# Eight squares added on VectorE ahead of one sum on TensorE, and the convolution's mean one step later, in a two-kind transformer stack

## The reference

```
def rms_norm_2(x, g, eps=1e-6):
    y = x * lax.rsqrt(jnp.mean(x * x, axis=-1, keepdims=True) + eps)
    return y * g

for i in range(2):
    h = x + 0.5 * swiglu(rms_norm_2(x, norm_ffn1[i]), w_ffn1_in[i], w_ffn1_out[i])
    u = rms_norm_2(h, norm_mix[i])
    q, k, v, c, g = jnp.split(u @ w_in[i], splits, axis=-1)
    ...
    y_attn = window_attention(q, k, v, sink[i], rel_bias) @ w_attn_out[i]
    c = c_val * jax.nn.sigmoid(c_gate)
    c = depthwise_conv(c, conv_w[i], conv_b[i])
    c = jax.nn.silu(layer_norm_2(c, conv_ln_g[i], conv_ln_b[i]))
    y_conv = c @ w_conv_out[i]
    h = h + (g_attn * y_attn + g_conv * y_conv) @ w_o[i]
    h = h + 0.5 * swiglu(rms_norm_2(h, norm_ffn2[i]), w_ffn2_in[i], w_ffn2_out[i])
    x = h + (p[i] @ w_pe_proj[i]) * jax.nn.sigmoid(rms_norm_2(h, norm_pe[i]) @ w_pe_gate[i])
```

## Time and profile before

| what | value |
|---|---|
| median of 3 runs | 2180.13 us (2177.9 to 2181.48) |
| the profiled execution's own time | 2180.48 us |
| its span, first to last instruction | 2178.4 us |
| mean granted TensorE clock | 0.999 |
| PE busy | 2154.0 us, 99% |
| DVE busy | 1677.4 us, 77% |
| ACT busy | 1264.3 us, 58% |
| HBM read | 409.42 MB, 189 GB/s over the span |

### The profile page before, as it was taken

The page is one execution under the profiler, slowest core; times in us unless marked ns, Lnnn a source line. Parts: engine busy times, 40 slices in busy tenths (PEclk is TensorE's granted clock), DMA queues, the critical chain, the costliest instruction groups (busy, mean ns, idle before and its releaser), DMA issues.

```text
span 2178.4 us, 38806 instructions
## 1 busy us (share of the span) xinstructions
PE 2154.0 (99%) x16092; PEld 1968.2 (90%) x16092; DVE 1677.4 (77%) x2609; ACT 1264.3 (58%) x2098; POOL 13.1 (1%) x20
## 2 busy tenths in 40 slices
PE   7999999999999999999999999999999999999999
PEld 6898999998998998998888999988898889998888
DVE  7877589887876678876787677888678766978875
ACT  4744656554755556555555557566565545676554
POOL 0000000000000000000000000000000000000000
PEclk9999999999999999999999999999999999999999
DMA  9544566777644467655555533555555554355554
GB/s 371 182 157 167 169 241 233 251 246 267 232 146 156 151 226 225 212 175 185 184 189 188 184 121 115 202 193 189 188 176 192 189 188 136 117 165 204 192 189 131
DMA packets 116225, 415.10 MB, mean 191 GB/s; under 512 B 13089, under 2 KB 16289, under 8 KB 115538
## 3 DMA queue, kind: packets, MB, share of 16 engines
q1 hardware_dynamic: 116050, 412.63, 56.4%
HBM read 409.42 MB, written 3.16 MB: 189 GB/s over the span
## 4 chain that ended last, share of the span: by engine, by line
PE 94%; DVE 2%; ACT 2%; DMA 2%; issue 0%; SPq 0%; ACTq 0%
PE bank L198 93%; DMA raw<-W 1%; ACT arena L250 1%; PE bank L202 1%; DVE arena L205 1%; DVE lo L205 1%; DMA xT<-x 0%; ACT hi L250 0%; DVE ada L222 0%; ACT L242 0%; DVE arena L213 0%; ACT L250 0%; DVE h L205 0%; SPq L195 0%; DVE ysl L205 0%
## 5 line engine op out<-in xcount | busy, mean ns | idle before, releaser
L198 PE MATMUL bank<-h,hi 128*128 128x256 f32 (+1 forms) x5344 | 1224.3, 314 | 0.0
L250 ACT ACTIVATE hi<-raw 128x1024 fp32r<-128x1024 f32 x656 | 689.1, 1056 | 572.6 <-PE bank L198 512.0
L198 PE MATMUL bank<-h,lo 128*128 128x256 f32 x3440 | 986.6, 287 | 2.9 <-DVE h L205 2.8
L198 PEld LDWEIGHTS bank<-h,hi 128*128 128x128 f32 x5344 | 881.3, 191 | 67.2 <-issue 2.6
L205 DVE TENSOR_TENSOR lo<-raw,hi 128x1024 fp32r<-128x1024 f32 x656 | 793.4, 1221 | 93.0 <-ACT hi L250 92.1
L198 PEld LDWEIGHTS bank<-h,lo 128*128 128x128 f32 x3440 | 655.3, 191 | 14.7 <-issue 7.1
L198 PE MATMUL bank<-act,hi 128*128 128x512 f32 x1056 | 370.0, 393 | 0.0
L198 PE MATMUL bank<-act,lo 128*128 128x256 f32 x1056 | 294.7, 279 | 0.0
L198 PEld LDWEIGHTS bank<-act,hi 128*128 128x128 f32 x1056 | 197.9, 187 | 47.2
L198 PE MATMUL bank<-arena 64*64 64x64 f32 (+7 forms) x2674 | 197.4, 271 | 3.0 <-ACT arena L250 2.7
L198 PEld LDWEIGHTS bank<-act,lo 128*128 128x128 f32 x1056 | 197.9, 187 | 0.0
(11 more groups left out here) (150 smaller groups left out, 1913.8 us busy)
## 6 DMA issues: line engine op xcount, KB each, us to landing
raw<-W SPq DMA_DIRECT2D x664, 512.0 KB, 3.4
ada<-WA SPq DMA_DIRECT2D x80, 512.0 KB, 3.6
arena<-WA SPq DMA_DIRECT2D x16, 512.0 KB, 14.6
p_projected<-arena SPq DMA_DIRECT2D x2, 1024.0 KB, 7.9
arena<-scr SPq DMA_DIRECT2D x16, 128.0 KB, 4.8
arena<-p_projected SPq DMA_DIRECT2D x2, 1024.0 KB, 4.9
xT<-x SPq DMA_DIRECT2D x2, 512.0 KB, 5.8
arena<-lora SPq DMA_DIRECT2D x2, 512.0 KB, 10.9
```

Of the source, the lines that this page charges most:

```text
L198: return self.done(lambda e: e.matmul(out, l, r, start=start, stop=stop, skip_group_check=True))
L250: return self.done(lambda e: e.activation(out, in_, f, scale=scale, **kw))
```

## The change

For the eight norms of the second kind DVE adds all eight squares: `summed(norm)` is 7 for them and stays 5 for the others. After the lower half of tile 7 DVE adds square 6 and then square 7 (for the first `f1`, also those of the final norm). On PE, `squares` then has a single matmul for such a norm, and a single one for the final norm. Only the last matmul of a sum now signals. In the convolution's chain, "mean" and all that follows it come one tick later.

```diff
+def summed(norm):
+    return 7 if norm and norm[0] in ("f1", "mx", "f2", "pl") else SUMMED
...
-    return s + ["next", ("mean",), "next", ("square",), "next", ("var",), "next", ("norm",), ("silu",), "next", ("split",)]
+    return s + ["next", "next", ("mean",), "next", ("square",), "next", ("var",), "next", ("norm",), ("silu",), "next", ("split",)]
...
-            def squares(norm, parts, final=False):
+            def squares(norm, final=False):
+                parts = ["sum"] + list(range(summed(norm) + 1, KD))
                 for m in parts:
-                    if m in (0, "sum"):
+                    if m == "sum":
                         take(STAT, ("stat", norm))
...
-                    pe.mm(statb[:, 0:256], C("ones"), src, m in (0, "sum"), m == 7).then_inc(pe_main, ("stat", norm, m))
+                    i = pe.mm(statb[:, 0:256], C("ones"), src, m == "sum", m == parts[-1])
+                i.then_inc(pe_main, ("stat", norm))
                 if final:
-                    for m in parts:
-                        if m == "sum":
-                            take(ONE, "stat2")
-                            pe.wait_ge(v_main, "fsq sum")
-                        else:
-                            pe.wait_ge(a_main, ("fsq", m))
-                        src = t256(ht, 0 if m == "sum" else m)
-                        pe.mm(adab[:, 256:512], C("ones"), src, m == "sum", m == 7).then_inc(pe_main, ("stat2", m))
+                    take(ONE, "stat2")
+                    pe.wait_ge(v_main, "fsq sum")
+                    pe.mm(adab[:, 256:512], C("ones"), t256(ht, 0), True, True).then_inc(pe_main, "stat2")
...
-                if norm and 2 <= m <= SUMMED + 1:
+                if norm and 2 <= m <= summed(norm) + 1:
                     add_square(norm, m - 1)
+                if m == summed(norm) == KD - 1:
+                    add_square(norm, m)
...
-                    v_main, ("sq part", norm, m), *([("sq sum", norm)] if m == SUMMED else []))
+                    v_main, ("sq part", norm, m), *([("sq sum", norm)] if m == summed(norm) else []))
```

More of the change, by code:

```diff
@@ L1128, in tensor_program @@
                     pe.wait_ge(v_main, ("start sq", 256))
-                    pe.mm(statb[:, 0:256], C("ones"), t256(sqb, 0), True, True).then_inc(pe_main, ("stat", norm, 7))
+                    pe.mm(statb[:, 0:256], C("ones"), t256(sqb, 0), True, True).then_inc(pe_main, ("stat", norm))
                     start()
@@ L1135, in tensor_program @@
                     p_proj(l, [0])
-                    squares(("n1", l), ["sum", 6, 7])
+                    squares(("n1", l))
                     p_proj(l, [1, 2, 3])
@@ L1206, in tensor_program @@
                         flips(ONE, [0])
-                    squares(("n2", l), ["sum", 6, 7])
+                    squares(("n2", l))
                     if l == 0:
@@ L1230, in tensor_program @@
                     ffn_in(i, l, [0, 1], [(k, n) for k in range(KD) for n in range(4)])
-                    squares((f"f{i}", l), ["sum", 6, 7], (i, l) == (1, 0))
+                    squares((f"f{i}", l), (i, l) == (1, 0))
                 elif what == "f":
@@ L1245, in tensor_program @@
                     if m == 0:
-                        squares(("mx", l), ["sum", 6, 7])
+                        squares(("mx", l))
                 elif what == "rcol":
@@ L1289, in tensor_program @@
                     if m == 0:
-                        squares(("pl", l), ["sum", 6, 7])
+                        squares(("pl", l))
             assert f.n == NBLK * BT, f.n
@@ L1410, in add_square @@
                     v.tt(t256(ht, 0), t256(ht, 0), t256(ht, m), ADD).then_inc(
-                        v_main, ("fsq part", m), *(["fsq sum"] if m == SUMMED else []))
+                        v_main, ("fsq part", m), *(["fsq sum"] if m == summed(norm) else []))
             def updates(kind, l, p, nk):
@@ L1864, in vector_program @@
                             v.wait_ge(v_main)
-                            v.wait_ge(pe_main, ("stat2", 7))
+                            v.wait_ge(pe_main, "stat2")
                             v.tt(var_t, var_t, adab[:, 256:512], MUL).then_inc(v_main, "final var", frees="stat2")
@@ L2041, in factor @@
             def factor(norm):
-                a.wait_ge(pe_main, ("stat", norm, 7))
+                a.wait_ge(pe_main, ("stat", norm))
                 a.act(var_t, statb[:, 0:256], ACT.Ln, bias=C("eps6")).then_inc(a_main, ("ln", norm), frees=("stat", norm))
```

## The result

The changed kernel takes 2186.96 us (median of 7 runs, 2186.52 to 2189.03), the kernel before 2179.67 (7 runs): 1.0033 times as long, with a 95% interval from 1.0024 to 1.0042. It is 7.3 us slower, and outside the range given. The span of the profiled executions goes from 2178.4 to 2185.2 us.

What follows compares the result with a forecast made beforehand. PE, busy 99% of the span, was taken to bound the kernel. 7.8 us gained from sums, less 0.7 at `pl` and 7.3 at the tails, gave -0.2: forecast 2180.7 us, no change, range 2173.5 to 2185.

Steps and rivals of the forecast that it cites:

- 18 x 0.433 = 7.8 us off PE: At eight norms and the final norm, two float32 sums each leave PE, 0.433 us apiece, 7.8 us in all.
- work taken off PE counts in full: Premise for the whole kernel: with PE busy 99% of the span, any work removed from it shortens the time fully.
- The tail's 7.3 us: Convolution's tail one tick later: PE waits 4.8 us per layer in place of 1.15, 7.3 more for two layers.
- at the variance: First tail wait, inside attention's projection: PE waits 0.76 us for DVE's variance sums in place of 1.15.
- at the projection: Second tail wait, at the convolution's projection: late ACT table loads delay the first lower half, PE waits 2.9 us.
- at its second piece: Convolution's projection, after 6 matmuls: PE waits 0.9 us more for the second lower half.
- in the output product: DVE leaves the tail late and costs PE 0.2 us a layer at the output product's fifth lower half.
- DVE late at the output product: Slower rival: DVE carries the tail's lateness into the output product, 2.4 us a layer, 2185.5 us; chance 0.14.
- `pl`'s wait: At the `pl` norm the sum waits for DVE's two adds: 0.35 us in each of two layers, 0.7.
- One load for Ln and Exp: Rival in the convolution's tail: Ln's table load serves Exp too, 1.28 us shorter a layer, 2178.1 us; chance 0.07.
- no loads: Rival in the convolution's tail: Ln and Exp find their table, 2.56 us shorter a layer, 2175.5 us; chance 0.12.

Runs made afterwards that it cites:

- squares_only: The changed kernel with the convolution's mean put back to its earlier tick, so only the squares differ from the kernel before; 2178.6 us, ratio 0.9996.
- two_sums_only: Changed kernel, mean at its earlier tick, six squares added and two float32 sums at the three norms with slow FFN stretches; 2174.51 us, ratio 0.9976.
- mean_only: The kernel before with only the convolution's mean one tick later, squares and sums as before; 2189.61 us, ratio 1.0044.
- table_late: The changed kernel with ACT's table request moved from behind the square to ahead of Ln; 2179.75 us, ratio 1.0002 to the kernel before.
- more_sums: The changed kernel with dummy sums on PE, making two, three and four ahead of the three slow FFN stretches; 2184.63 us, ratio 1.0021.

## Why the prediction was wrong

- **"18 x 0.433 = 7.8 us off PE"** is the step that failed. The sums are off PE: the mixer's norm takes 0.25 from its first record to the next ordinary matmul (1231.94 to 1232.19) where it took 1.11 (1233.87 to 1234.98). But the step, and the premise "work taken off PE counts in full" ahead of it, took for granted that what PE does behind a sum takes as long as before. In three FFN stretches it doesn't: 3 x 2.1 = 6.3 us given back at places where no engine waits. squares_only (1.0 us gained of 7.1 forecast) and two_sums_only (5.0, with three sums left standing) show it from both sides. That the same matmuls have a second pace stood in the trace of before, where no wait and no count shows it: PE's first kind of block has it (rows in the last section).
- **The tail's 7.3 us** was right term by term where the clock stayed up, in layer 1. Lost time ahead of a matmul, beyond a step of 0.12: 0.73 at the variance (1353.07 - 1352.22; 0.76 forecast); in layer 1, 2.64 at the projection (1935.41 - 1932.65; 2.9), 0.77 at its second piece (1936.96 - 1936.07; 0.9) and 0.2 in the output product (0.2). With 0.2 for the slower first matmuls behind the waits that is 4.5, and 3.4 without the 1.15 of before, where 3.65 was forecast. Layer 0 lost 3.9. That the two come to 7.3 to the tenth is luck, for layer 0 has 0.5 of the clock in it; by medians the later mean costs 8.4 beside the squares (2186.96 - 2178.6) and 10.0 without them. The rival nearest in time, DVE late at the output product (2185.5), isn't what happened: PE lost 0.2 there, not 2.4.
- **The clock** was not in the forecast. In layer 0 it fell for 3.4 us, but in that time PE reached its second piece so late that the second wait was gone, so that it cost 3.9 - 3.4 = 0.5 there. In mean_only the fall came later, towards the end of the second wait, and a tail cost 4.5, 1.1 more than without a fall.
- **`pl`'s wait** was right: the last product's matmul starts at 1589.42, the sum at 1589.91, 0.37 beyond a step of 0.12, and 0.49 in layer 1 (2159.64 to 2160.25); 0.35 forecast. The other norms show no wait.
- **One load for Ln and Exp.** The Trainium skill (ScalarE: Activation LUTs, section "Table sets: the hidden batching unit") has one load serve Ln and then Exp. The trace differs where Ln brings its own load: Exp brings another (1356.45 and 1358.24). It agrees where the set with both was requested right ahead (table_late). So the rule's condition here is who asked for the set, and the rival "no loads" was one moved line away: the chance it got was for the change as written, where the loads came.

Together, by the starts: tails 3.9 + 3.4 = 7.3, pace 6.3, sums with the waits at `pl` -6.7 (read at each norm, some 0.87 less for every two sums), and the -0.2 from ahead of the second kind of block: the 6.8 of the spans. The forecast had 7.3 and -7.1 and no third term.

Open is what in PE makes the second pace. Shown is that one float32 sum ahead of an FFN stretch brought it in 15 of 17 and two or more never did at a stretch's start; that DVE's work, the clock and the sum's place by one matmul have no part in it; that a sum midway can end it or leave it; and that it also comes with no sum near. Whether it is the number of sums or the time for which they hold PE (0.43 us, or 0.87 and more) no run tells apart. What tells the two exceptions in table_late from the rest was not found; chance from one execution to the next isn't ruled out, for a product that is the same in all kernels here also came at either pace.

## What to carry to other kernels

Where PE is 99% busy, work taken off it counts only if the matmuls around it keep their pace: compare the distance of starts over a whole stretch in both traces, not only waits and counts. A step moved in ACT's order can put another function between a requested table and its use; move the request with it. And a wait of PE may cost more than itself: behind those of 2.5 us the clock fell in four tails of six.

## What the runs showed of the hardware that was not expected

- The same alternation of 128x256 and 128x512 float32r matmuls runs at one of two paces, 346.7 or 353.3 ns a tile, at a granted clock of 1.00 in both, and keeps one for 300 tiles. It isn't bound to this change, nor to float32 sums: in the first kind of block, where nothing was changed, the last 55 of the 64 tiles of layer 0's output product (`wout`) follow a wait for DVE and no sum. They ran at 353.3 to 353.4 in five of the twelve profiles, that of the kernel before among them, and at 346.7 in the others. PE's timeline before:

```profile
318.01 0.38 PE L198 MATMUL bank<-h,lo 128*128 128x256 f32 x1 [1.45 <-DVE h L205]
...
318.46 0.28 PE L198 MATMUL bank<-h,lo 128*128 128x256 f32 x1
...
337.90 0.28 PE L198 MATMUL bank<-pfh,lo 128*128 128x256 f32 x1
```

and after:

```profile
318.04 0.28 PE L203 MATMUL bank<-h,lo 128*128 128x256 f32 x1
...
337.11 0.28 PE L203 MATMUL bank<-pfh,lo 128*128 128x256 f32 x1
```

55 tiles take 19.44 us before and 19.07 after.

- After PE had stood still for 2.5 us the granted clock went to 1.2 GHz for 3.4 us in four of the six tails with that wait (one of two in the changed kernel and in more_sums, both in mean_only); after waits of 0.6 us alone it never did.
- A request for a table set puts out the one that the next function would have used: without it Tanh needed no load, so that one moved request saved three loads of 1.28 us a layer.
